# Forget gates of a two-block model: which operand of the matmul stands still and which moves

## What is computed

```python
h = rmsnorm(x, mix_pre_gain[0])
proj = h @ w_in                       # 1024 x (4*1024 + 16)
f_logit = proj[..., 4 * D_ATT:]       # 16 columns
log_f = log_sigmoid(f_logit + b_f)
c = cumsum(log_f, axis=1)             # along the tokens
s = q @ k^T * scale + c[query] - c[key]
```

## Time and profile before

| | us |
|---|---|
| median of 3 runs | 1266.86 |
| lowest, highest | 1266.7, 1274.25 |
| the profiled execution, its time | 1265.16 |
| its span in the profile | 1263.4 |
| TensorE busy | 1194.1 (95%) |
| VectorE busy | 799.0 (63%) |
| ScalarE busy | 592.2 (47%) |
| mean granted clock of TensorE | 0.968 |

### The profile page before, as it was taken

The page is one execution under the profiler, slowest core; times in us unless marked ns, Lnnn a source line. Parts: engine busy times, 40 slices in busy tenths (PEclk is TensorE's granted clock), DMA queues, the critical chain, the costliest instruction groups (busy, mean ns, idle before and its releaser), DMA issues.

```text
span 1263.4 us, 17533 instructions
## 1 busy us (share of the span) xinstructions
PE 1194.1 (95%) x7210; PEld 974.3 (77%) x7210; DVE 799.0 (63%) x1297; ACT 592.2 (47%) x905; POOL 121.3 (10%) x124
## 2 busy tenths in 40 slices
PE   7899799999999999999999999999988898999997
PEld 6767589797788888888867777887867776888785
DVE  5646664545866778554645688677776968555644
ACT  6465233223546556345544564454473336534531
POOL 0303141410000000000000000000321510000000
PEclk9998799999999999998989999999999799999999
DMA  8522111112455455553512265455533043655551
GB/s 292 177 100 84 34 50 54 48 34 100 154 183 181 174 183 176 183 183 119 168 51 99 100 237 180 153 194 187 187 126 122 4 159 125 208 190 183 189 192 55
DMA packets 49665, 177.45 MB, mean 140 GB/s; under 512 B 5648, under 2 KB 6288, under 8 KB 49328
## 3 DMA queue, kind: packets, MB, share of 16 engines
q1 hardware_dynamic: 49584, 176.32, 40.9%
HBM read 175.25 MB, written 1.05 MB: 140 GB/s over the span
## 4 chain that ended last, share of the span: by engine, by line
PE 80%; DVE 10%; ACT 5%; POOL 2%; issue 1%; DMA 1%; SPq 0%; DVEq 0%; ACTq 0%
PE wps L2583 20%; PE wps L2585 20%; PE wps L2584 20%; PE tps L2572 4%; DVE wlo L1757 2%; PE tps L2770 2%; PE tps L2629 2%; PE tps L2788 2%; PE tps L2779 1%; ACT whi L1384 1%; PE tps L2950 1%; PE tps L2882 1%; DVE arena L1982 1%; POOL arena L2476 1%; ACT over L1669 1%
## 5 line engine op out<-in xcount | busy, mean ns | idle before, releaser
L1757 DVE TENSOR_TENSOR wlo<-raw,whi 128x1024 fp32r<-128x1024 f32 (+1 forms) x322 | 388.6, 1231 | 197.0 <-ACT whi L1384 195.7
L2583 PE MATMUL wps<-whi,a_hi 128*128 128x512 f32 (+1 forms) x1008 | 407.2, 404 | 14.9 <-DVE a_lo L1779 8.4
L2585 PE MATMUL wps<-wlo,a_hi 128*128 128x512 f32 (+1 forms) x1008 | 396.4, 393 | 0.0
L2584 PE MATMUL wps<-whi,a_lo 128*128 128x512 f32 (+1 forms) x1008 | 396.2, 393 | 0.0
L1384 ACT ACTIVATE whi<-raw 128x1024 fp32r<-128x1024 f32 (+1 forms) x322 | 325.3, 1050 | 53.0 <-PE wps L2585 51.0
L2583 PEld LDWEIGHTS wps<-whi,a_hi 128*128 128x128 f32 x1008 | 193.4, 192 | 59.8 <-issue 11.1
L2585 PEld LDWEIGHTS wps<-wlo,a_hi 128*128 128x128 f32 x1008 | 192.3, 191 | 41.2
L2584 PEld LDWEIGHTS wps<-whi,a_lo 128*128 128x128 f32 x1008 | 193.4, 192 | 36.9
L2583 PE MATMUL wps<-whi,f_hi 128*128 128x512 f32 x264 | 104.6, 396 | 0.0
L2585 PE MATMUL wps<-wlo,f_hi 128*128 128x512 f32 x264 | 104.2, 395 | 0.0
L2584 PE MATMUL wps<-whi,f_lo 128*128 128x512 f32 x264 | 104.2, 395 | 0.0
(11 more groups left out here) (382 smaller groups left out, 1399.2 us busy)
## 6 DMA issues: line engine op xcount, KB each, us to landing
raw<-in_w_dn SPq DMA_DIRECT2D x22, 512.0 KB, 3.3
raw<-in_w_0dn SPq DMA_DIRECT2D x22, 512.0 KB, 3.3
raw<-in_w_1dn SPq DMA_DIRECT2D x22, 512.0 KB, 3.2
raw<-in_w_ua SPq DMA_DIRECT2D x20, 512.0 KB, 3.3
raw<-in_w_ub SPq DMA_DIRECT2D x20, 512.0 KB, 3.4
raw<-in_w_0ug SPq DMA_DIRECT2D x20, 512.0 KB, 3.3
raw<-in_w_0uu SPq DMA_DIRECT2D x20, 512.0 KB, 3.3
raw<-in_w_1ug SPq DMA_DIRECT2D x20, 512.0 KB, 3.3
```

What stands on the lines that cost most here:

```text
L1757: V.tensor_tensor(t.wlo[n % NR][:, 0:w], t.raw[n % NR][:, 0:w], t.whi[n % NH][:, 0:w].bitcast(F32), ALU.subtract).then_inc(m.done(s.dve_lo ...
L2583: T.matmul(o, xh, wh, start=first, stop=False)
L2584: T.matmul(o, xl, wh, start=False, stop=False)
L2585: mm = T.matmul(o, xh, wl, start=False, stop=last)
```

## The change

The roles in the forget product are turned round. A new piece `forget_split` repeats the 16 weight columns eight times, to 128, and splits them into high and low parts `wfh` and `wfl` (ScalarE copies 128 x 1024 with a broadcast read, VectorE subtracts 128 x 1024). `forget_mm` loads 128 weight columns and moves the 256 tokens, in three products for each of the 8 pieces: 24 fp32r matmuls, and the result is already heads by tokens. `forget_row` makes the root a row: the root column of each half of the tokens, repeated to 16 columns, is loaded and the unit matrix moves, twice. `forget_take` is then a ScalarE copy of that row to SBUF and a VectorE product of it with the logits. `forget` 0 adds the bias in place. The transposes (`forget_T`) are gone. The job has two steps more: split behind fq1/0, product and row behind fq1/1, take behind fq1/2, bias behind fq1/3, and so on, each later piece two slabs further on than before. One PSUM bank is used where two were, and it is held meanwhile.

```diff
--- before.py
+++ after.py
@@ -794,17 +794,19 @@
     def forget_gates():
         for _ in range(4):
             yield
+        emit("forget_split")
+        yield
         b = bank()
+        b.held = True
         emit("forget_mm", b.name, b.free, tuple(e for k in range(8) for e in both_sides(main.tok[k])))
         while norm["tok"] is None:
             yield
-        emit("forget_take", b.name, norm["tok"])
-        b.free = (("forget_take", 1),)
-        b = bank()
-        emit("forget_T", b.name, b.free)
+        emit("forget_row", b.name, norm["tok"])
         yield
-        emit("forget", 0, b.name)
-        b.free = (("forget_in",),)
+        emit("forget_take", b.name)
+        b.free, b.held = (("forget_take",),), False
+        yield
+        emit("forget", 0, None)
         yield
         emit("forget", 1, None)
         yield
@@ -1196,6 +1198,7 @@
     with ExitStack() as s4:
         t.fq, t.fk, t.fv, t.fgt = (sb(name, [P, 2, D], F32, s4) for name in ("fq", "fk", "fv", "fgt"))
         t.wf = sb("wf", [P, 8, 16], F32, s4)
+        t.wfh, t.wfl = sb("wfh", [P, 8, 8, 16], F32R, s4), sb("wfl", [P, 8, 8, 16], F32R, s4)
         t.fprob = [sb(f"fprob{i}", [P, 384], F32, s4)[:, :] for i in range(3)]
         t.fprobT = [sb(f"fprobT{i}", [P, 384], F32, s4)[:, :] for i in range(2)]
         t.fc = sb("fc", [16, 4, S], F32, s4)
@@ -1596,19 +1599,21 @@
         last_square[:] = [("post_square", i, c, j)]
 
     @part
-    def forget_take(b, r):
-        act.wait_ge(*m.at("root", r))
-        act.wait_ge(*m.at("forget_mm"))
-        for j in range(2):
-            activate(t.cqt[:, j, :], t.bank[b][:, 16 * j:16 * j + 16], ACT.Copy, scale=t.st[:, 2 + j:3 + j]).then_inc(
-                m.done(s.act_out, "forget_take", j), 1)
+    def forget_split():
+        act.wait_ge(*m.at("wf"))
+        activate(t.wfh[:, :, :, :], t.wf[:, :, :].unsqueeze(2).to_broadcast([P, 8, 8, 16]), ACT.Copy).then_inc(m.done(s.act_out, "forget_wh"), 1)
+
+    @part
+    def forget_take(b):
+        act.wait_ge(*m.at("forget_row"))
+        activate(t.fc[:, 3, :], t.bank[b][0:16, S:2 * S], ACT.Copy).then_inc(m.done(s.act_out, "forget_root"), 1)
 
     @part
     def forget(i, b):
         f0, f1 = t.fc[:, 0, :], t.fc[:, 1, :]
         if i == 0:
-            act.wait_ge(*m.at("forget_T"))
-            activate(f0, t.bank[b][0:16, 0:S], ACT.Identity, bias=vcol(t, "b_f", 0, 16)).then_inc(m.done(s.act_out, "forget_in"), 1)
+            act.wait_ge(*m.at("forget_take"))
+            activate(f0, f0, ACT.Identity, bias=vcol(t, "b_f", 0, 16)).then_inc(m.done(s.act_out, "forget_in"), 1)
         elif i == 1:
             act.wait_ge(*m.at("forget_abs"))
             activate(f1, f1, ACT.Exp, scale=-1.0).then_inc(m.done(s.act_out, "forget_exp"), 1)
@@ -2143,6 +2148,17 @@
         V.tensor_scalar(t.fgq[:, :], vcol(t, "fox_g", 0), 0.125, None, ALU.mult).then_inc(m.done(s.dve_out, "fgq"), 1)
 
     f0, f1, f2, f3 = (t.fc[:, i, :] for i in range(4))
+
+    @part
+    def forget_split():
+        dve.wait_ge(*m.at("forget_wh"))
+        V.tensor_tensor(t.wfl[:, :, :, :], t.wf[:, :, :].unsqueeze(2).to_broadcast([P, 8, 8, 16]), t.wfh[:, :, :, :].bitcast(F32), ALU.subtract).then_inc(m.done(s.dve_out, "forget_wl"), 1)
+
+    @part
+    def forget_take(b):
+        dve.wait_ge(*m.at("forget_mm"))
+        dve.wait_ge(*m.at("forget_root"))
+        V.tensor_tensor(f0, t.bank[b][0:16, 0:S], f3, ALU.mult).then_inc(m.done(s.dve_out, "forget_take"), 1)
 
     @part
     def forget(i, b):
@@ -2873,23 +2889,24 @@
 
     @part
     def forget_mm(b, freed, ready):
+
         wait_all(freed)
         wait_all(ready)
-        pe.wait_ge(*m.at("wf"))
+        pe.wait_ge(*m.at("forget_wl"))
+        o, (ah, al) = t.bank[b][:, 0:S], t.acts["a"]
+        for k in range(8):
+            wh, wl = (w[:, k, :, :].rearrange("p a h -> p (a h)") for w in (t.wfh, t.wfl))
+            T.matmul(o, wh, ah[:, k, :], start=k == 0, stop=False)
+            T.matmul(o, wh, al[:, k, :], start=False, stop=False)
+            mm = T.matmul(o, wl, ah[:, k, :], start=False, stop=k == 7)
+        mm.then_inc(m.done(s.pe_side, "forget_mm"), 1)
+
+    @part
+    def forget_row(b, r):
+        pe.wait_ge(*m.at("root", r))
         for j in range(2):
-            for k in range(8):
-                for n_, a in enumerate(t.acts["a"]):
-                    mm = T.matmul(t.bank[b][:, 16 * j:16 * j + 16], a[:, k, j * P:(j + 1) * P].bitcast(F32), t.wf[:, k, :],
-                                  start=(k == 0 and n_ == 0), stop=(k == 7 and n_ == 1))
-        mm.then_inc(m.done(s.pe_side, "forget_mm"), 1)
-
-    @part
-    def forget_T(b, freed):
-        wait_all(freed)
-        for j in range(2):
-            pe.wait_ge(*m.at("forget_take", j))
-            mm = turn(t.bank[b][0:16, j * P:(j + 1) * P], t.cqt[:, j, :])
-        mm.then_inc(m.done(s.pe_side, "forget_T"), 1)
+            mm = T.matmul(t.bank[b][0:16, S + j * P:S + (j + 1) * P], t.st[:, 2 + j:3 + j].to_broadcast([P, 16]), t.con[:, 0:P], start=True, stop=True)
+        mm.then_inc(m.done(s.pe_side, "forget_row"), 1)
 
     @part
     def forget_q(b, freed):
```

## The result

The changed kernel takes 1257.22 us (median; 1255.0 to 1261.08), the kernel before 1266.7 in the same comparison (1264.63 to 1274.25). The ratio is 0.9927, with a 95% interval of 0.9903 to 0.9951: 9.2 us less, between 6 and 12. Forecast were 1258.0 and "within 1%".

The account below looks back on a forecast made before the run. TensorE, four fifths of the chain that ended last, was taken to bound the kernel; 2.86 + 0.25 + 0.1 + 0.4 + 0.1 = 3.71 in place of 12.37 us, 8.7 less, gave 1258.0 us, range 1255 to 1263.

Parts of the forecast that it names:

- The loss before, 12.37 us: TensorE between fq1/0 and fq1/1: 11.02 us until fq1/1 starts plus 1.35 for its slow first six products.
- The product, 2.86: New forget product on TensorE: 24 fp32r matmuls of 256 columns at 0.119 us each, loads hidden, 2.86 us.
- The rival with unhidden loads: New forget product: loads not hidden, 24 x 0.212 = 5.1 us, 2.2 us more, total 1260.4; chance 0.12.
- the one with plain f32: New forget product runs as plain f32, 0.625 us a matmul, 15.0 us: 3.5 us slower than before, 1270.4; chance 0.03.
- The wait for `wfl`, 0.4: TensorE reaches forget_mm before VectorE's subtraction is through and waits 0.4 us, bounds 0 and 0.8.
- Row and changes of form, 0.25 + 0.1: Root's row, two plain f32 matmuls: 0.25 us with the entry; changes of form at both ends: 0.1 us.
- four records in 0.22 us with the entry: Price of the root's row, taken from L2838's matmuls: 0.25 us with the entry, 0.5 at half that pace.
- fk1/2, 0.1: VectorE's half of slab fk1/2's split is over at 5.5 where TensorE wants it at 5.44: 0.1 us, bounds 0 and 0.6.
- The two table loads: Loads of 1.28 us each ahead of exp and ln, now in fk0/0 and fk0/1: hidden, by 1.0 us.
- Total: TensorE's new costs sum to 3.71 us in place of 12.37: 8.7 us less, forecast time 1258.0.
- Given back behind: Late splits, waiting transposes of q or a new clock fall eat the gain: 1260.5 to 1265 us; chance 0.12.
- the clock behind the new product: TensorE's granted clock stays at 1.00 right through from fq1/1 to fk0; a half clock after the matmuls would be wrong.

Follow-up runs that it names:

- e3: The changed kernel with the 16 weight columns not repeated, so the split works on 128 columns in place of 1024: 1256.55 us, ratio 0.9895.
- e4: The changed kernel with forget_split one step earlier, ahead of fq0's takes: 1257.44 us, ratio 0.9901.
- e7: The changed kernel with the root's row ahead of the forget product, in a PSUM bank of its own: 1258.35 us in one execution.
- e2: The changed kernel without forget_split: product turned, but 16 plain f32 matmuls of 256 columns with 16 unrepeated weight columns loaded: 1263.37 us, ratio 0.9966.
- e6: The kernel before with its forget product in two pieces of 16 matmuls, behind fq1/0 and fq1/2: 1265.85 us in one execution.

## Why the prediction was right

**The loss before, 12.37 us.** Right in size, and now split: 4.36 of it was the clock (four pieces), the rest is work and chain. The prediction counted the half clock as part of what goes; had it argued from busy time alone, the 6.67 / 31 = 0.215 us a load in the slow stretch of the earlier trace rows would have looked like the cost of the instruction.

**The product, 2.86.** 2.94 measured, at 0.118 us each where 0.119 was extended from two rows; what is more comes from the first gap, 0.23, which belongs to the wait ahead of it. The rival with unhidden loads (0.212 each, 5.1) and the one with plain f32 (0.625) fall: none of the 23 gaps is over 0.12 but the first. The Trainium skill (TensorE: Matmul & The Clock Gate, Part 3, The mechanism) would have had the unhidden case, since every load here uses all rows; this trace does not agree, at 0.118 us a matmul. The same section also lets a load that goes to a background weight buffer run ahead, and a reader who goes by that sentence would have had the hidden case. The same page's section Back-to-back issue gap gives 0.109 for 256 columns; the traces show 0.114 to 0.118.

**The wait for `wfl`, 0.4.** 0.39 measured. The walk through the queues was some 2.2 us early in absolute time only because this execution's first part was longer; counted from the start of fq1/0 it holds: `wfl` ready at 5.78 us behind the start of fq1/0 (570.21 - 564.43), forecast 5.80 (568.05 - 562.25). e3 and e4 each take it away and gain 0.5, with the gap behind it.

**Row and changes of form, 0.25 + 0.1.** This term was mis-sized: 0.63 measured, and 0.10 behind it in the products' first gap, so 0.73 for 0.35. The step that failed is "four records in 0.22 us with the entry": the price was taken from matmuls in the middle of a run of their own kind, while a lone pair pays 0.08 on entering (0.31 from the product to the row in e7) and 0.55 until the next start. A row that changes form would have been the better price; the bound of 0.5 that I kept for it was too low as well.

**fk1/2, 0.1.** 0.03 measured. The sums of squares of fk0 come 0.8 us later counted from fk0's start, not 1.0, and VectorE is through with fk1/2's half 5.3 us behind fk1's start where 5.5 was forecast and TensorE wants it at 5.44. The two table loads are hidden as said; VectorE's halves for fk0/3 and fk1/0 end 7.2 and 10.0 us behind fk0's start, forecast 7.15 and 9.85.

**Total.** 4.09 for 3.71, 8.3 saved for 8.7. That the median is within 1 us of 1258.0 all the same is partly luck: the forecast was 0.4 us too good in the middle part, and executions of the changed kernel reach from 1255.0 to 1261.08. The interval of the ratio, 3 us either way, also shows that the kernel can be measured more finely than the 1% (12.7 us) that the prediction took for the limit. The clock is 1.00 from fq1/1 to fk1's end, as forecast. "Given back behind" did not come: 620 to 760 us is granted 0.95 as in the earlier trace rows, and the last part of after lies 1.9 us below and 2.0 above before's. That the total can move with the clock elsewhere was right to keep in the range: the same code ahead of the change took between 562.25 and 567.13 us.

**Argued too shortly** was the clock behind the new product. The prediction let it stay at 1.00 without pricing the case that it falls, and no row of before could have shown which way it goes. It stays at 1.00 in e2's 6.92 us as well, and falls 3.2 to 3.6 us behind the start of each piece of the old product in e6; so the length of the new product, 2.94, would have been no safe argument in either direction.

## What to carry to other kernels

Read the granted clock not only over a side job but over the work behind it: TensorE is busy throughout in the old product, and the products after it pay for it. Where such a job ends in half clock, turn its operands round so that the many columns move, or cut it and lay the pieces between the large products: four pieces gave half of the gain for a dozen lines and two gave nothing, so the size of the piece must be measured. A small helper matmul in another form costs more than its records: price it from a lone one, with both changes of form, and fill a wait with it if there is one.

## What the runs showed of the hardware that was not expected

- Sixteen plain f32 matmuls with 128 x 16 columns (32 full loads, some 3.5 us) were followed by 3.4 and 6.8 us at half clock, the second time from their last matmuls on; eight of them (1.8 us) by none, four times over. TensorE was busy throughout when the clock fell.
- A plain f32 matmul of 256 columns takes 0.431 us with 16 columns loaded (e2), and 0.625 with 128 loaded (where every second one has 32 rows in place of 128), in two records each time. The 0.19 more would fit two wide loads that are not hidden (0.105 each by the prediction's estimate); this is not shown, since no run changed the load's width alone in plain f32; in fp32r 16 or 128 loaded columns make no difference.
- The fp32r 256-column matmul has two paces, 0.114 and 0.118 us, with either load width and at clock 1.00: after held 0.118 throughout, e7 held 0.114 with the same operands, and e3 and after's second profile went from 0.118 to 0.114 on the way. What decides it stays open; it is worth 0.1 us here.
- A broadcast read of 16 columns eight times costs ScalarE and VectorE what a dense read of 1024 costs (1.04 and 1.23 us).
